# Paged attention: page requests moved to the start of the next group's values, behind a sequence's addition

## The reference

```python
ckv_past = cache_ckv[l, page_table].reshape(db, past_len, KV_LORA)      # 256 values per token
kr_past = cache_krope[l, page_table].reshape(db, past_len, MLA_ROPE)    # 32 values per token
q_lat = jnp.einsum('bthn,lhn->bthl', q_nope, w_uk)
s_past = (jnp.einsum('bthl,bpl->bhtp', q_lat, ckv_past)
          + jnp.einsum('bthr,bpr->bhtp', q_rope, krope_past))
...
p = jax.nn.softmax(s, axis=-1).astype(c_kv.dtype)
lat = (jnp.einsum('bhtp,bpl->bthl', p[..., :P], ckv_past) + ...)
```

## Time and profile before

| | |
|---|---|
| median of 3 runs | 1910.0 us |
| the profiled execution | 1910.69 us |
| its span, first to last instruction | 1908.8 us |
| TensorE busy | 1827.8 us, 96% |
| VectorE busy | 1216.4 us, 64% |
| ScalarE busy | 569.3 us, 30% |
| GpSimd busy | 567.0 us, 30% |
| software DMA queue (the pages) | 75.50 MB in 7168 packets |
| granted TensorE clock, mean | 0.987 |

### The profile page before, as it was taken

One profiled execution on the slowest core, in us unless ns is written; L12 is line 12 of the kernel. 1 busy time (PEld: TensorE's weight loads), 2 busy tenths in 40 slices (PEclk: granted clock), 3 DMA queues, 4 the chain that ended last, 5 costly groups with the idle time before them and its releaser, 6 DMA issues.

```text
span 1908.8 us, 34292 instructions
## 1 busy us (share of the span) xinstructions
PE 1827.8 (96%) x14782; PEld 1587.6 (83%) x14782; DVE 1216.4 (64%) x1563; ACT 569.3 (30%) x978; POOL 567.0 (30%) x392
## 2 busy tenths in 40 slices
PE   7999999898998999989998899999999999999998
PEld 6989889885664444449997699999999999999998
DVE  5587776565877887874332756873675276375475
ACT  5222321353553454452121531120111021011026
POOL 2222122240001343422224533333332333333530
PEclk9999999998999999999999999999999999999999
DMA  7121122141002888853134511112111211211202
GB/s 245 45 57 45 47 57 45 39 123 48 1 1 91 324 320 314 315 188 104 30 89 143 177 56 45 46 39 61 45 41 42 63 39 34 61 45 43 79 23 92
DMA packets 162307, 176.72 MB, mean 93 GB/s; under 512 B 21982, under 2 KB 146932, under 8 KB 157772
## 3 DMA queue, kind: packets, MB, share of 16 engines
q1 hardware_dynamic: 146240, 93.54, 16.7%
q0 software_dynamic: 7168, 75.50, 10.5%
q10 hardware_dynamic: 8750, 5.49, 1.0%
HBM read 161.33 MB, written 13.27 MB: 91 GB/s over the span
## 4 chain that ended last, share of the span: by engine, by line
PE 87%; DVE 7%; issue 3%; ACT 1%; DMA 1%; POOL 1%; SPq 0%; ACTq 0%; DVEq 0%; POOLq 0%
PE PS L799 21%; PE PS L801 20%; PE PS L800 20%; PE PS L1120 4%; PE PS L836 4%; PE PS L1162 3%; PE PS L1014 2%; PE PS L1107 1%; PE PS L1142 1%; PE PS L1055 1%; PE PS L1131 1%; PE PS L881 1%; PE PS L987 1%; PE PS L1335 1%; PE PS L1337 1%
## 5 line engine op out<-in xcount | busy, mean ns | idle before, releaser
L737 POOL CAST whi<-wraw 128x1024 fp32r<-128x1024 f32 (+4 forms) x142 | 137.4, 968 | 915.8 <-PE PS L801 860.0
L799 PE MATMUL PS<-BH,whi 128*128 128x344 f32 x1152 | 368.9, 320 | 0.0
L800 PE MATMUL PS<-BL,whi 128*128 128x344 f32 x1152 | 367.1, 319 | 0.0
L801 PE MATMUL PS<-BH,wlo 128*128 128x344 f32 x1152 | 367.0, 319 | 0.0
L739 POOL TENSOR_TENSOR wlo<-wraw,whi 128x1024 fp32r<-128x1024 f32 (+4 forms) x142 | 311.2, 2192 | 11.4
L800 PEld LDWEIGHTS PS<-BL,whi 128*128 128x128 f32 x1152 | 216.2, 188 | 0.5 <-issue 0.5
L799 PEld LDWEIGHTS PS<-BH,whi 128*128 128x128 f32 x1152 | 216.2, 188 | 0.5 <-issue 0.5
L801 PEld LDWEIGHTS PS<-BH,wlo 128*128 128x128 f32 x1152 | 216.2, 188 | 0.0
L799 PE MATMUL PS<-XH,whi 128*128 128x344 f32 x528 | 179.0, 339 | 3.4 <-DVE XL L1911 3.4
L2391 DVE TENSOR_TENSOR XT<-PS,XT 128x1032 f32<-128x1032 f32 x48 | 59.2, 1233 | 175.9 <-PE PS L801 175.8
L800 PE MATMUL PS<-XL,whi 128*128 128x344 f32 x528 | 170.1, 322 | 0.0
(11 more groups left out here) (451 smaller groups left out, 3713.5 us busy)
## 6 DMA issues: line engine op xcount, KB each, us to landing
wraw<-in_w_up_dram SPq DMA_DIRECT2D x44, 512.0 KB, 3.9
wraw<-in_w_in_dram SPq DMA_DIRECT2D x20, 512.0 KB, 4.0
wraw<-in_w_down_dram SPq DMA_DIRECT2D x24, 256.0 KB, 2.9
wraw<-in_w_down_dram SPq DMA_DIRECT2D x16, 320.0 KB, 3.3
xt_kept<-XT SPq DMA_DIRECT2D x1, 4128.0 KB, 12.8
XT<-xt_kept SPq DMA_DIRECT2D x1, 4128.0 KB, 13.9
xstage<-in_x_prompt_dram SPq DMA_DIRECT2D x8, 512.0 KB, 10.4
wraw<-in_w_out_dram SPq DMA_DIRECT2D x8, 512.0 KB, 4.2
```

The source lines that it names most:

```text
L737: gp.tensor_copy(hi, raw).then_inc(w_hi_done, 1)
L799: pe.matmul(out, wh[:, t, 0:m], hi[:, tile(t), s], start=(t == first), stop=False)
L800: pe.matmul(out, wh[:, t, 0:m], low, start=False, stop=False)
L801: ins = pe.matmul(out, wl[:, t, 0:m], hi[:, tile(t), s], start=False, stop=(t == last))
```

## The change

The request of group g gets a second wait, and the addition of a finished sequence is put ahead of the request of the same step.

```diff
                 elif g >= SLOTS:
                     full(gp, ("go", g - SLOTS))
+                    gp.wait_ge(half_turned, g - SLOTS + 2)
...
                     for g in range(SLOTS + GT - NG):
+                        if g >= SLOTS and (g - SLOTS) % NG == NG - 1:
+                            sequence_values(gp, step, (g - SLOTS) // NG)
                         if g < GT:
                             load_pages(g)
-                        if g >= SLOTS and (g - SLOTS) % NG == NG - 1:
-                            sequence_values(gp, step, (g - SLOTS) // NG)
```

## The result

The changed kernel takes 1898.24 us (median of 4 runs, 1896.97 to 1899.27) against 1909.67 us for the kernel before in the same session (4 runs, 1908.47 to 1912.11): ratio 0.9943, 95% interval 0.9929 to 0.9957. It is 11 us faster, less than half of the 25 us that I forecast. The profiled execution took 1899.27 us with a span of 1897.5.

What follows compares the result with a forecast made beforehand. TensorE's own sequence was taken as the bound. Removing the stall (33.2 us), less spill (5.7) and late requests behind additions (2.6), gave 24.9 us off 1910.69: 1886 us, range 1875 to 1911.

Steps and rivals of the forecast that it cites:

- The bound: TensorE carries 87% of the chain, so a change pays only where it shortens TensorE's own sequence.
- the steps with 128 rows: Values and `sum_scores` use all 128 partitions; a request starting under them was taken to cost 0.
- The turn waits for ScalarE's exponential: Sign of being right: TensorE's turn L836 waits for ScalarE's exponential, as in the undisturbed 6.29 us period.
- Pages land in time: Moved requests leave a lead of 11.5 or 10.2 us against a landing of 8.5; cost 0.
- The step on the addition: On GpSimd, 6 requests start later behind an addition put ahead of them, 0.44 us each: 2.6 us lost.
- what was said of leaving it behind: On GpSimd's queue, an addition left behind the request would be held by the new wait; no size given.
- nothing moves: Rival: the window pauses all of TensorE wherever it falls, or isn't tied to the request; 1910.7 us, chance 0.14.
- the start of the request: On GpSimd, the moved request starts 0.15 us after T, the start of a group's values, 5.44 us later than before.
- the spill: The part of the disturbed window still falling on row tiles in `part_scores`: 0.21 us per group, 5.7 us in 27.
- the window: TensorE's row-tile matmuls are disturbed from 1.66 to 2.85 us after the start of `rc`, 1.23 us per group.
- The slower rival: `rk` has its own window, falling in `part_scores` after the move, up to 0.85 us per group; 1934 us, chance 0.12.
- partial stall: Rival: `sum_scores`' small matmuls are held too, about 0.8 us per group left; gain 11.6 us, 1899 us, chance 0.24.

Runs made afterwards that it cites:

- E8: A separate kernel computing no outputs: TensorE runs one kind of matmul per stream, 17 streams, while GpSimd issues no, one or two DMAs; span 244.6 us.
- E2: The kernel before with the new wait alone, the addition staying behind the request; 1913.45 us, ratio 1.0032.
- E3: The changed kernel with the request waiting for the end of TensorE's turn of the weights instead of ScalarE's copy; 1894.12 us, ratio 0.9937.
- E4: The changed kernel with the request waiting for the end of `sum_scores` instead of ScalarE's copy; 1938.39 us, ratio 1.0168.
- E6: The kernel before with the two DMAs of a request exchanged, `rk` first; 1909.95 us.
- E7: The kernel before without the `rk` DMA of groups 5 and up, which keep old rotary keys; 1886.33 us.
- E5: The changed kernel with E3's signal and the request placed between the addition's second and third operations; 1893.62 us, ratio 0.9929; measured again 1889.99 us, ratio 0.9911.

## Why the prediction was right or wrong

**Right.** The bound: TensorE's own sequence, a stall of 1.23 us per period tied to the request, 33.2 us in all, only in row tiles. All 27 disappeared from their place; the steps with 128 rows cost nothing under the hold, and E8 shows it for both kinds. The turn waits for ScalarE's exponential again. Pages land in time. The step on the addition was 2.6 us and measured 2.4, in part by luck: five requests are late by it and not six, and each costs 0.36 to 0.54 us where I had 0.44. E2 confirms what was said of leaving it behind. The rival "nothing moves" is out, and with it what I concluded from the rule of the Trainium skill ("SBUF — State Buffer", section "Terms"), that the gaps must have another cause that stays. The rule itself speaks of DMA and engine accesses; E8 bears it out for traffic, and whether an access is what holds TensorE during the issue no run shows.

**Wrong: the start of the request.** The failed step is "with GpSimd's 0.30 us the request starts at T + 0.15". It starts at T + 0.63, 0.77 us after ScalarE's copy ends. The 0.30 holds for the kernel before, where the DMA's only wait is its own: by the semaphore times that the trace records (none of the views prints them) TensorE's signal comes at 731.52 and `rc` starts at 731.78, 0.26 us later, as for all 27 requests. The change gives the request a second condition, and that wait is an instruction of its own ahead of the DMA: ScalarE's signal comes at 732.83, the wait ends at 732.87, and `rc` starts at 733.59, 0.76 us after the signal, as for 21 of the 22 requests that don't start right behind an addition. It is not the engine that signals: E3 and E4 wait a second time for TensorE, and there too `rc` starts 0.76 us after the signal (720.70 to 721.46, 746.88 to 747.64); E6 and E7, with one wait, have 0.26. So I carried the wake-up of a DMA that waits by itself to one behind a wait instruction, which costs 0.50 us more. Row tiles begin at T + 2.79, so the spill is not 0.21 but 0.68 us: 27 x 0.67 = 18.1 us instead of 5.7, a loss of 12.4 of the 15.2 us by which the forecast of 24.9 missed the 9.7 of the stage. E3 tests it the other way: with `rc` at T + 0.13 the period is 6.46 to 6.50, the "about 6.5" of the prediction.

**Wrong in its reason, not in its sum: the window.** I gave it to `rc`, 1.66 to 2.85 us after its start. It is two holds, one per DMA, from the start of `rc` to 1.6 us after that of `rk`. The end is the same instant; only E4, where the beginning falls on row tiles too, tells the sum apart (2.36 us per group). The slower rival had half of this right: `rk` holds TensorE by itself. It erred on when.

**Missing: the gaps in the values**, 2.8 us. No term stood for them. In the kernel before hardly any shows (periods of 7.47 to 7.63 us), though such packets come there, about 3 us after the values' start in the first groups. They are the rest of the 15.2 us.

The rival "partial stall" gave 1899 us, nearly the time measured, for the wrong reason: nothing is lost under `sum_scores` (0.86 us before and after).

## What to carry to other kernels

Before moving a request by a wait, look at how it will wait. Here a DMA of GpSimd's that carries its only wait started 0.26 us after the signal, and one behind a separate wait 0.76 us after it, and half a microsecond per group was half of the gain that was forecast. Of two waits of which the later includes the earlier, as in E3 (both on TensorE's one counter), one could be left out; no run tried it. An indirect DMA from GpSimd costs TensorE about 1.3 us of dense small-tile issue from the start of its record, and nothing under the matmuls with 128 rows that were tried, so place it there whole, both DMAs of a pair. And if a stall sits at a fixed distance from two events, move each by itself before giving it to one.

## What the runs showed of the hardware that was not expected

- An indirect DMA issued by GpSimd holds a dense stream of 32-row tiles over all 16 tiles for 1.29 to 1.33 us (a pair: 2.80 to 2.85 us); two plain DMAs from the same queue, recorded within 1.12 us, don't.
- GpSimd starts an indirect DMA 0.26 us after the signal if the DMA carries the wait itself, and 0.76 us after it if a wait instruction stands ahead, whether ScalarE or TensorE signals.
- TensorE can stop in the middle of its values, for 0.89 to 1.54 us in the three chains shown. The stops end 2.16 to 2.49 us after the start of an instruction packet, and 128 added waits move their place. They make periods of 7.6 to 8.4 us in E5's version.
